# A two-block transformer step on one core: the relative-position bias is spread over the partitions by TensorE instead of by DRAM-to-DRAM copies

## The reference, cut to what matters

```python
off = np.arange(3 * blk)[None, :] - blk - np.arange(blk)[:, None]
for gi, (window, dil) in enumerate(DIL_GROUPS):          # (128,1), (512,4), (2048,16)
    bt = rel_bias[_t5_bucket(off * dil)]                 # rel_bias is (32, 12)
    group_bias.append(jnp.transpose(bt[:, :, hs], (2, 0, 1)))
...
logits = jnp.einsum('brnqhc,brnkhc->brnhqk', qr, kw) * (hd ** -0.5) + bias
logits = jnp.where(mask[:, None], logits, NEG)
```

## Time and profile before

| | |
|---|---|
| median of 3 runs | 1919.54 us (1917.04 to 1920.42) |
| profiled execution, its own time | 1920.42 us |
| span of the profiled execution, first to last instruction | 1918.6 us |
| PE busy | 96% of the span |
| DVE, ACT, POOL busy | 43%, 40%, 32% |
| mean granted TensorE clock | 0.982 of full |
| moved by DMA | 145.77 MB, 77 GB/s over the span |

### The profile page before, as it was taken

One profiled execution on the slowest core, in us unless ns is written; L12 is line 12 of the kernel. 1 busy time (PEld: TensorE's weight loads), 2 busy tenths in 40 slices (PEclk: granted clock), 3 DMA queues, 4 the chain that ended last, 5 costly groups with the idle time before them and its releaser, 6 DMA issues.

```text
span 1918.6 us, 22756 instructions
## 1 busy us (share of the span) xinstructions
PE 1843.5 (96%) x9622; PEld 1459.8 (76%) x9622; DVE 824.8 (43%) x1338; ACT 764.7 (40%) x1218; POOL 606.0 (32%) x190
## 2 busy tenths in 40 slices
PE   8999989999999999998999999989989999998997
PEld 5777989997888888877888888877665477765556
DVE  7656645741331230112670153165336642724653
ACT  5985554443432332223331222233436523434541
POOL 3444161132333233443354443424230024321001
PEclk9999989999999999999999999989999999999999
DMA  5121110133433222322222322213120012111001
GB/s 202 66 88 23 21 25 23 45 126 132 127 99 105 87 101 88 110 88 88 70 106 88 110 88 96 102 44 148 61 88 1 1 66 102 66 66 44 1 1 44
DMA packets 37494, 145.77 MB, mean 76 GB/s; under 512 B 3155, under 2 KB 15835, under 8 KB 23440
## 3 DMA queue, kind: packets, MB, share of 16 engines
q1 hardware_dynamic: 18944, 122.94, 18.0%
q10 hardware_dynamic: 18448, 21.37, 3.9%
HBM read 142.14 MB, written 5.30 MB: 77 GB/s over the span
## 4 chain that ended last, share of the span: by engine, by line
PE 91%; DVE 3%; ACT 3%; POOL 1%; issue 1%; DMA 0%; POOLq 0%; SPq 0%; DVEq 0%; ACTq 0%
PE bank L409 55%; PE bank L1077 7%; PE bank L613 5%; PE bank L420 4%; PE bank L2049 3%; PE bank L2070 3%; PE bank L2056 2%; PE bank L1504 1%; PE bank L1480 1%; ACT w_part L367 1%; PE bank L662 1%; PE bank L1998 1%; PE bank L817 1%; PE bank L1113 1%; ACT WK L2179 1%
## 5 line engine op out<-in xcount | busy, mean ns | idle before, releaser
L409 PE MATMUL bank<-x_part,w_part 128*128 128x512 f32 x3264 | 758.1, 392 | 0.8 <-DVE x_part L577 0.6
L409 PEld LDWEIGHTS bank<-x_part,w_part 128*128 128x128 f32 x3264 | 610.0, 188 | 134.2 <-issue 7.5
L2496 POOL TENSOR_TENSOR w_part<-RAW,w_part 128x2048 fp32r<-128x2048 f32 (+1 forms) x90 | 402.8, 4478 | 816.6 <-ACT w_part L367 813.9
L2496 POOL TENSOR_TENSOR w_part<-WK,w_part 128x2048 fp32r<-128x2048 f32 (+1 forms) x30 | 126.2, 4207 | 361.1 <-ACT w_part L367 361.1
L367 ACT ACTIVATE w_part<-RAW 128x2048 fp32r<-128x2048 f32 (+1 forms) x90 | 166.7, 1852 | 176.7 <-PE bank L409 138.3
L409 PE MATMUL bank<-f_part,w_part 128*128 128x512 f32 x768 | 174.4, 389 | 0.0
L409 PEld LDWEIGHTS bank<-f_part,w_part 128*128 128x128 f32 x768 | 144.2, 188 | 29.9
L1077 PE MATMUL bank<-WK 128*128 128x128 f32 (+1 forms) x1056 | 116.6, 274 | 1.6 <-DVE WK L1334 1.5
L1077 PEld LDWEIGHTS bank<-WK 128*128 128x128 f32 (+1 forms) x1056 | 114.2, 190 | 2.8 <-DVE WK L1334 1.6
L2049 PE MATMUL bank<-WK 64*128 64x512 f32 (+3 forms) x256 | 83.2, 600 | 9.7 <-ACT STAT L2165 9.7
L933 DVE SCALAR_TENSOR_TENSOR WK<-bank,COL,WK 128x510 f32<-128x510 f32 (+1 forms) x96 | 71.6, 748 | 44.7 <-ACT WK L880 42.1
(11 more groups left out here) (282 smaller groups left out, 2335.2 us busy)
## 6 DMA issues: line engine op xcount, KB each, us to landing
RAW<-wts SPq DMA_DIRECT2D x84, 1024.0 KB, 4.8
WK<-wts SPq DMA_DIRECT2D x24, 1024.0 KB, 4.8
WK<-scratch ACTq DMA_DIRECT2D x16, 256.0 KB, 2.7
WK<-decay_rows ACTq DMA_DIRECT2D x14, 256.0 KB, 6.4
RAW<-wts SPq DMA_DIRECT2D x6, 512.0 KB, 3.4
WK<-wts SPq DMA_DIRECT2D x6, 512.0 KB, 3.4
scratch<-bias_rows ACTq DMA_DIRECT2D x4, 768.0 KB, 8.2
WK<-xT SPq DMA_DIRECT2D x4, 512.0 KB, 6.0
```

The source lines that it names most:

```text
L409: mm = pe.eng.matmul(b[:, :], W[w][:, k, c:c + P], src[x][k], start=start and k == 0 and n == 0, stop=stop and k == kn - 1 and n == 2)
L2496: eng.tensor_tensor(low_part(i), raw_part(i), high_part(i).bitcast(F32), ALU.subtract).then_inc(w_split, 1)
```

## The change

The table's row is spread over the 128 partitions by the matmul itself. For each head index `hh`, four matmuls with a stationary operand of 33x128, in which one column of `relb` is repeated 128 times (a step of zero), give 128 equal rows of 1536 values: two matmuls of 512 columns for group 0 and one of 256 for each of the groups 1 and 2. That is 16 matmuls in 4 visits instead of 3 matmuls in 3 visits. The first visit is ahead of q0, the others stand where the three matmuls stood. ACT copies each of the 16 results into `BR` (now full 128 rows) and its queue writes `BR` to `scratch[hh]` as one SBUF-to-DRAM store. `BR` is single: before ACT writes it for the next `hh` it waits for the store before, and before the first value projection is copied into the same words it waits for the last store. The DRAM tensor `bias_rows`, the three small stores and the four DRAM-to-DRAM copies are gone. `bias_tiles` is unchanged.

```diff
-            def bias_row(j):
-                b = job(("bias", j))
-                E.matmul(b[0:12, :], RELB[0:33, :], SEL[0:33, j * S:(j + 1) * S], start=True, stop=True).then_inc(*pe.did(("pe", ("bias", j))))
+            def bias_rows(hh):
+                for j, (g, lo, n) in enumerate(((0, 0, 512), (0, 512, 512), (1, 1024, 256), (2, 1280, 256))):
+                    b = job(("bias", hh, j))
+                    E.matmul(b[:, 0:n], RELB[0:33, 4 * g + hh:4 * g + hh + 1].broadcast_to([33, P]), SEL[0:33, lo:lo + n], start=True, stop=True)\
+                        .then_inc(*pe.did(("pe", ("bias", hh, j))))
...
+            bias_rows(0)
             for hh in range(4):
...
                 else:
-                    bias_row(0)
+                    bias_rows(1)
                 project(hh, "q", 1)
...
                 else:
-                    bias_row(1)
+                    bias_rows(2)
                 project(hh, "q", 2)
...
                 else:
-                    bias_row(2)
+                    bias_rows(3)
...
-            def bias_row(j):
-                act.wait_ge(*at(("pe", ("bias", j))))
-                A.activation(BR[0:12, j * S:(j + 1) * S], ps(("bias", j))[0:12, :], ACT.Copy).then_inc(*act.did(free=("bias", j)))
-
-            def bias_to_memory():
+            def bias_rows(hh):
+                for j, (lo, n) in enumerate(((0, 512), (512, 512), (1024, 256), (1280, 256))):
+                    act.wait_ge(*at(("pe", ("bias", hh, j))))
+                    if hh:
+                        act.wait_ge(bias_out[hh - 1], 16)
+                    A.activation(BR[:, lo:lo + n], ps(("bias", hh, j))[:, 0:n], ACT.Copy).then_inc(*act.did(free=("bias", hh, j)))
                 act.wait_ge(*act.last())
-                for g, (lo, n) in enumerate(((0, 1024), (1024, 256), (1280, 256))):
-                    A.dma_start(bias[:, lo:lo + n], BR[4 * g:4 * g + 4, lo:lo + n]).then_inc(bias_rows_out, 16)
-
-            def bias_spread():
-                act.wait_ge(bias_rows_out, 48)
-                for hh in range(4):
-                    A.dma_start(scratch[hh], bass.AP(tensor=bias.tensor, offset=hh * 1536, ap=[[0, P], [1, 1536]])).then_inc(bias_out[hh], 16)
+                A.dma_start(scratch[hh], BR).then_inc(bias_out[hh], 16)
...
+            bias_rows(0)
             for hh in range(4):
...
                     if not hh:
-                        bias_row(g)
-                if not hh:
-                    bias_to_memory()
+                        bias_rows(g + 1)
...
-                    elif not hh:
-                        bias_spread()
                 for r in range(2):
                     if not hh:
                         bias_tiles(r)
+                if not hh:
+                    act.wait_ge(bias_out[3], 16)
```

More of the change, by code:

```diff
@@ L173, with build @@
 NTAB = 3840
-def build(nc, xT, cols, base, gdnc, tabs, wgate, relb, sel, small, wts, out, scratch, rows, bias, old):
+def build(nc, xT, cols, base, gdnc, tabs, wgate, relb, sel, small, wts, out, scratch, rows, old):
     subs = sub_list()
@@ L319, in build @@
         small_in = [sem(f"small_weights_in{l}") for l in range(LAYERS)]
-        bias_rows_out = sem("bias_rows_out")
-        bias_out = [sem(f"bias_spread{i}") for i in range(4)]
+        bias_out = [sem(f"bias_rows_out{i}") for i in range(4)]
         bias_in = [sem(f"bias_in{i}") for i in range(2)]
@@ L325, in build @@
         rows_in = [sem(f"decay_rows_in{u}") for u in range(8)]
-        for s in [rows_out, bias_rows_out, *rows_in, *w_in_slot, w_split, const_in, gdnc_in, wgate_in, sel_in, *x_in, x_again, tabs_in, *small_in, *bias_out, *bias_in, out_done]:
+        for s in [rows_out, *rows_in, *w_in_slot, w_split, const_in, gdnc_in, wgate_in, sel_in, *x_in, x_again, tabs_in, *small_in, *bias_out, *bias_in, out_done]:
             byname[s.name] = s
@@ L2533, in make_program @@
         rows = nc.dram_tensor("decay_rows", (2 * HEADS, S), F32, kind="Internal").ap()
-        bias = nc.dram_tensor("bias_rows", (4, 1536), F32, kind="Internal").ap()
-        old = build(nc, out=out, scratch=scratch, rows=rows, bias=bias, old=old, **t)
+        old = build(nc, out=out, scratch=scratch, rows=rows, old=old, **t)
     return nc
```

## The result

The changed kernel takes 1931.49 us (median of 4 runs, 1930.92 to 1935.39), the kernel before 1918.29 us beside it (4 runs): a ratio of 1.0068, with a 95% interval of 1.0048 to 1.0089. It is slower by 13.2 us, where +10.2 was forecast, and the time lies inside the range. The profiled execution took 1935.57 us (above the range), with a span of 1933.8. With it and eight further executions the changed kernel was timed 13 times: 1924.50 to 1935.57 us, six of them with a mean granted clock of 0.977, two of 0.984. The kernel before stayed within 1914.69 and 1922.93 us beside the experiments, apart from a single execution of 3741.52 us that is left out of all ratios.

What follows compares the result with a forecast made beforehand. The prediction took PE to bound the kernel, busy for 1843.5 of 1918.6 us. Removed matmuls -3.4, added +12.1 and the bank wait +1.5 gave +10.2 us on a median of 1919.54: 1929.7 us, range 1926.5 to 1934.0.

Steps and rivals of the forecast that it cites:

- PE is the bound; nothing hides an addition: Whole kernel: any microsecond added to PE's program adds one to the kernel, unless PE was waiting there.
- PE's work, +8.7 us: Bias visits among the projections: 16 matmuls and their turns add 12.1 us, three removed visits give back 3.4.
- a turn: At each of the 4 bias visits: changing row count and back costs PE 0.32 us, 1.3 us in all.
- Weight loads inside a visit hidden: Between matmuls of one bias visit: loading the stationary operand adds no time; if not hidden, 1.9 us more.
- The bank that changes hands, +1.5 us: First output projection of lay0 and lay1: shifted rotation makes PE wait for bank 6's reader, 0.77 us each.
- Stores hidden: Bias stores beside the projections: each lands after 5 us, and PE waits only if it takes over 9.0.
- everything between shifted by 8.7 us and otherwise alike: Changed profile between the bias visits and the output projections: the same work, only 8.7 us later.
- bare loads: Rival at the bias visits: weight loads not hidden between matmuls, +12.1 us in all, 1931.6 us; chance 14%.
- slow stores: Rival at the bias stores: PE comes to wait for them, +14 us in all at 11 us each; chance 7%.
- The likeliest case: Whole kernel: the forecast itself, +9.5 to +11 us, likeliest 1929.7 us; chance 58%.

Runs made afterwards that it cites:

- rows64: The changed kernel with its bias matmuls over 64 rows, rows 33 to 63 zero in both operands; ratio 1.0050 to the kernel before.
- before_rows128: The kernel before with its three bias matmuls over 128 rows, zeros in 33 to 127; 1918.67 us in a single execution.
- rotation_only: The kernel before with the rotation over the 8 banks moved on by 5 at the end of stage dil, nothing else; ratio 1.0013.
- stores_twice: The changed kernel with each 768 KB store issued twice and all waits for both; ratio 1.0075 to the kernel before.
- rows128: The changed kernel with its bias matmuls over all 128 rows, rows 33 to 127 zero in both operands; ratio 1.0045 to the kernel before.
- singles: The changed kernel with its 16 bias matmuls put one by one inside the first four projections; ratio 1.0079 to the kernel before.
- pairs: The changed kernel with its bias matmuls in pairs inside the first four projections, after 6 and 18 of 24 matmuls; ratio 1.0068 to the kernel before.
- rows128_rotation_back: The changed kernel with bias matmuls over 128 rows, zeros in 33 to 127, and the bank rotation moved on by 3; ratio 1.0050 to the kernel before.

## Why the prediction was right, and what it missed

- **PE is the bound; nothing hides an addition.** Right. PE is busy for 51.00 of 51.00 us from 440 to 491 us after.
- **PE's work, +8.7 us.** Right in size: +8.4 us measured in rows64, which has all of it and no falls. Two parts of it were off against each other: 256 columns cost 0.62 - 0.19 = 0.43 us and not the 0.48 of the row that I took, and a turn costs 0.4 us and not 0.32. The cause that I gave for the turn, the row count, was wrong in part: before_rows128 has it with 128 rows.
- **Weight loads inside a visit hidden.** Right: 2.77 us is the 2.58 us of the columns and one way out, so nothing is added between the four matmuls. The sentence of the Trainium skill that I had weighed (page "TensorE: Matmul & The Clock Gate", section "Part 3: Packing small matmuls — row/col tiling", loads overlap only across row groups) would have given 3.4 us more, and the trace disagrees with it here. The same section also lets a load into the background weight buffer go ahead of running matmuls, which the forecast did not weigh and with which the trace agrees. The load records of the bias matmuls last 0.19 us each and not the 0.107 of the page.
- **The bank that changes hands, +1.5 us.** Right in mechanism, shown alone by rotation_only; 0.89 us instead of 0.77 in each layer, 1.8 us together. Most of the 0.12 us more is the release: the forecast allowed 0.06 us, for which it has no row, and the trace has 0.15, the same that lies between 1543.85 and 1544.00 in the earlier trace rows.
- **Stores hidden.** Right: 3.3 us against the 5 taken; at 4.5 us in stores_twice still no wait.
- **The step that failed:** "everything between shifted by 8.7 us and otherwise alike". The term that the sum lacked is the granted clock. I read 1.00 and, without a row for four such matmuls in a row, carried it over to a stage in which PE would be as busy as before. The four visits made the clock fall behind them, 1.6 us each, 6.3 us in the profiled execution. rows64 and rows128 take it away with the copies and stores in place; singles and pairs take it away by splitting the visits; in stores_twice more traffic changes nothing. Each has one profile, but the runs agree: the mean granted clock is 0.977 in 6 of the 13 executions of the changed kernel, and between 0.980 and 0.983 in all 15 of rows64, rows128 and rows128_rotation_back. In the medians not all of it shows (13.2 us, and 15.2 between the two profiled spans, not 8.4 + 1.8 + 6.3 = 16.5). The falls don't come every time, and the other stages scatter by 2 us and more from one execution to the next. How the 3.3 us divide between the two was not measured.
- **What was luck.** The sum lacked a term of up to 6.3 us, and the median still lay in the range, because the range had room for bare loads and slow stores, neither of which came. The likeliest case, +9.5 to +11 us, did not come either. The median of 1931.49 us is what the bare loads would have given (1931.6), and only the trace tells the two apart: inside a visit nothing is added, and behind it the projections take 1.6 us more. The changed kernel's own scatter reaches past both ends of the range.

The Trainium skill, page "TensorE: Matmul & The Clock Gate", section "Part 1: The HAM clock gate", says that the gate goes by how busy the engine has been lately. In this trace "busy" in the sense of the profile does not tell when it falls: PE was busy for every microsecond around the falls. What stays open is how the clock weighs a part-filled array, since 33 rows for 2.8 us let it fall and 64 rows did not. Why the fall comes behind some visits and not others is open too.

## What to carry to other kernels

Where TensorE is the bound, cost an added matmul by its columns, but ask also how many of the array's rows it fills: here 2.8 us of 33-row matmuls in a row could halve the clock of the dense work behind them for some 3.5 us. Padding the operands with zeros to 64 or 128 rows added nothing to PE's time and kept the clock in every profile here; whether it makes the whole kernel faster than the changed one is not clear of the scatter (1.0045 with an interval of 1.0033 to 1.0057, against 1.0048 to 1.0089). When buffers or banks are given out in rotation, count the requests that an edit adds modulo the number of banks, and look where the rotation meets a fixed assignment far downstream. Compare stretch by stretch when the total scatters by more than the part in question.

## What the runs showed of the hardware that I had not expected

- The granted clock fell to 1.2 GHz behind 2.8 us of matmuls with 33 of 128 rows although PE never idled; single matmuls (0.86 us) and pairs (1.7 us) of the same kind did not do it, nor did 64 rows, of which 31 were zero, nor 128, of which 95 were, each in one profiled execution.
- A change of operand shape costs 0.27 us there and back at 12 columns of weights and 0.4 us at 128 columns with part-filled rows, and nothing between full shapes.
- A short wait behind the removed copies is not theirs. In the profiled execution of rotation_only, which still has them, the chain passes through a weight tile around 490 us:

```profile
487.38 6.12 DMA RAW<-wts
493.50 0.02 issue
493.52 1.92 ACT w_part L367
```

PE then waits 0.56 us at L1480, where it waited 0.35 us before. It looks as if the copies had held up the tile. But the last of the four was issued at 464.9 us, and the slowest landed 13.5 us after its issue, so all had landed by 478.4. This tile was issued at 487.38, right behind the PE projection that ends at 487.36. The changed kernel, which has no such copies, waits 0.4 us at the same logits matmul (L1481). So nothing here shows a gain from their removal.
